# Router logits from unscaled tokens, four experts' rows gathered by rank, GpSimd products behind the bonus products

## The reference, cut to what matters

```python
x = x + y_mix @ w_out[l]
h = rms_norm_2(x, norm_ffn_w[l])          # h = x * rsqrt(mean(x^2) + eps) * w
...
g_logits = xt @ rg_w + rg_b               # 8 groups
g_sel = argmax(g_logits); g_gate = softmax(g_logits)[g_sel]
e_logits = (xt @ re_w + re_b)[group g_sel]   # 8 experts in a group
top_p, top_i = top_k(softmax(e_logits), 2)
gates = g_gate * top_p / sum(top_p)
...
hid = silu(xblk @ w_gate[e]) * (xblk @ w_up[e])    # 1024 -> 512
y = hid @ w_down[e]                                # 512 -> 1024
```

## Time and profile before

| | before |
|---|---|
| median of 3 runs | 1588.18 us (1586.01 to 1589.27) |
| the profiled execution, its own time | 1582.05 us |
| its span, first to last instruction | 1580.3 us |
| busy PE / DVE / ACT / POOL | 1154.5 / 364.5 / 218.0 / 74.7 us |
| DMA | 463.21 MB, mean 293 GB/s |

### The profile page before, as it was taken

The page is one execution under the profiler, slowest core; times in us unless marked ns, Lnnn a source line. Parts: engine busy times, 40 slices in busy tenths (PEclk is TensorE's granted clock), DMA queues, the critical chain, the costliest instruction groups (busy, mean ns, idle before and its releaser), DMA issues.

```text
span 1580.3 us, 35719 instructions
## 1 busy us (share of the span) xinstructions
PE 1154.5 (73%) x15903; PEld 839.9 (53%) x15903; DVE 364.5 (23%) x993; ACT 218.0 (14%) x600; POOL 74.7 (5%) x124
## 2 busy tenths in 40 slices
PE   7988799888998787786556655666656666665665
PEld 4867368554687574764444444444444444444443
DVE  2455024731324724311010111111111110101111
ACT  1044000530013320110000000000000000000000
POOL 1100001000100311000000000000000000000000
PEclk9996899999998889898897889888888888889888
DMA  9740136205030006699999999999999999999997
GB/s 289 278 148 1 30 110 220 80 0 191 38 107 1 2 4 247 285 375 429 429 427 430 427 429 428 429 429 427 430 426 430 427 430 428 428 429 427 430 426 324
DMA packets 68872, 463.21 MB, mean 293 GB/s; under 512 B 14645, under 2 KB 18134, under 8 KB 44246
## 3 DMA queue, kind: packets, MB, share of 16 engines
q1 hardware_dynamic: 64784, 459.76, 70.7%
q10 hardware_dynamic: 4038, 2.72, 0.6%
HBM read 461.41 MB, written 1.05 MB: 293 GB/s over the span
## 4 chain that ended last, share of the span: by engine, by line
DMA 51%; PE 7%; DVE 1%; issue 1%; ACT 0%; POOLq 0%; SPq 0%; POOL 0%; DVEq 0%
DMA weight_slots<-in_exp_w_down_dram 51%; PE bank L2150 4%; PE bank L2141 1%; PE bank L2130 1%; PE bank L2167 0%; PE bank L2111 0%; PE bank L2104 0%; ACT work_region L2081 0%; SPq L1990 0%; DVE normed_features L2277 0%; DVE normed_tokens L2216 0%; POOLq L2028 0%; DVE tokens L2331 0%; DVE normed_features L2274 0%; DVE normed_features L2248 0%
## 5 line engine op out<-in xcount | busy, mean ns | idle before, releaser
L2141 PE MATMUL bank<-weight_slots,work_region 128*32 128x128 f32 x5504 | 201.3, 308 | 130.6 <-DMA weight_slots<-in_exp_w_up_dram 102.8
L2141 PEld LDWEIGHTS bank<-weight_slots,work_region 128*32 128x32 f32 x5504 | 173.9, 124 | 157.1 <-DMA weight_slots<-in_exp_w_up_dram 113.6
L2150 PE MATMUL bank<-weight_slots,work_region 128*32 128x256 f32 x1376 | 115.0, 491 | 91.3 <-DMA weight_slots<-in_exp_w_down_dram 91.3
L2141 PE MATMUL bank<-work_region 128*32 128x128 f32 x2688 | 95.2, 302 | 62.3 <-DMA work_region<-in_exp_w_up_dram 50.7
L2150 PEld LDWEIGHTS bank<-weight_slots,work_region 128*32 128x32 f32 x1376 | 59.1, 134 | 133.3 <-issue 98.6
L2141 PEld LDWEIGHTS bank<-work_region 128*32 128x32 f32 x2688 | 82.7, 121 | 75.6 <-DMA work_region<-in_exp_w_up_dram 56.0
L2081 ACT COPY work_region<-bank 128x256 f32<-128x256 f32 x64 | 23.8, 372 | 609.5 <-PE bank L2150 609.5
L2297 DVE TENSOR_SCALAR work_region<-work_region 128x128 f32<-128x128 f32 x128 | 38.7, 345 | 294.1 <-PE bank L2158 293.0
L2308 DVE TENSOR_TENSOR work_region<-work_region,bank 128x128 f32<-128x128 f32 x64 | 23.9, 373 | 288.1 <-PE bank L2141 288.1
L2150 PE MATMUL bank<-work_region 128*32 128x256 f32 x672 | 58.0, 503 | 44.1 <-DMA work_region<-in_exp_w_down_dram 44.1
L515 PE MATMUL bank<-weight_slots,normed_features 128*128 128x512 f32 (+2 forms) x256 | 87.0, 500 | 2.2 <-DVE normed_features L701 2.2
(11 more groups left out here) (416 smaller groups left out, 1279.6 us busy)
## 6 DMA issues: line engine op xcount, KB each, us to landing
weight_slots<-in_exp_w_up_dram SPq DMA_DIRECT2D x43, 2048.0 KB, 41.0
weight_slots<-in_exp_w_down_dram SPq DMA_DIRECT2D x43, 2048.0 KB, 40.6
weight_slots<-in_exp_w_gate_dram SPq DMA_DIRECT2D x43, 2048.0 KB, 41.7
work_region<-in_exp_w_gate_dram SPq DMA_DIRECT2D x21, 2048.0 KB, 41.7
work_region<-in_exp_w_up_dram SPq DMA_DIRECT2D x21, 2048.0 KB, 41.0
work_region<-in_exp_w_down_dram SPq DMA_DIRECT2D x21, 2048.0 KB, 40.9
weight_slots<-in_w_in_dram SPq DMA_DIRECT2D x16, 2048.0 KB, 9.4
weight_slots<-in_w_out_dram SPq DMA_DIRECT2D x6, 2048.0 KB, 8.0
```

The lines of the kernel that those rows point to most:

```text
L2141: mm = nc.tensor.matmul(B[bank][BLK * j:BLK * (j + 1), 0:P], xt[u][:, c], w[u][:, c, j * P:(j + 1) * P], start=c == 0, stop=c == KC - 1, t ...
L2150: mm = nc.tensor.matmul(B[7][BLK * j:BLK * (j + 1), 0:256], hidt[u][:, BLK * k:BLK * (k + 1)], w_down[u][:, k, j * 256:(j + 1) * 256], sta ...
```

## The change

Three things are changed.

1. **Router logits.** The norm's gain is multiplied into the router's weights by GpSimd in the mixer (one more DMA, `route_gain`, on ACT's queue; one GpSimd product of 128x576 after the q and k norm). PE transposes the unscaled tokens `X` and forms the logits at the mixer's end, ahead of the barrier; `rstd` enters as a factor when DVE adds the bias. DVE still makes `XN`, now ahead of the barrier too.
2. **First four experts.** DVE forms `first_pick`, a 128x32 selection for each of the first four experts and each half of the tokens, straight from the ranks. PE gathers these 128 rows from `XN` (4 matmuls of 128x512) and transposes them (8). The sorted selection is formed later, and PE gathers the sorted list in four quarters, one behind each of the steps 0 to 3, which are written out ahead of the loop. GpSimd's windows begin at expert 4.
3. **GpSimd behind the bonus.** The two `ends` products wait for the four `rk` products, where they waited for `scaled` 5.

```diff
             inv_root(rsq, ssq, 1.0 / HD, EPS, S["qk_ss"], 1, S["qk_rstd"])
+            pool.wait_ge(mem["router_in"], 16 * N_ROUTER)
+            nc.gpsimd.tensor_tensor(w_route, w_route, shape(mem["route_gain"].unsqueeze(2), P, KC, NGROUP + NE), ALU.mult).then_inc(mem["route_ready"], 1)
...
-            pool.wait_ge(S["scaled"], 5)
+            pool.wait_ge(S["rk_ready"], CT)
             nc.gpsimd.tensor_tensor(ends(ei), ends(kx), by, ALU.mult).then_inc(S["ends_ready"], 1)
...
                 nc.scalar.activation(junk[m], X[:, m * D:(m + 1) * D], ACT.Square, accum_out=ss[:, m:m + 1]).then_inc(S["ss_ready"], 1)
+                for b in range(2):
+                    act.wait_ge(S["h_transposed"], 2 * MT + 2 * m + b + 1)
+                    nc.scalar.copy(ht[:, 4 * b:4 * b + 4, m * P:(m + 1) * P], view(B[RAW_BANK[m][b]][:, :], 4, P)).then_inc(S["ht_ready"], 1)
...
+            pe.wait_ge(mem["route_ready"], 1)
+            for m in range(MT):
+                pe.wait_ge(S["ht_ready"], 2 * MT + 2 * (m + 1))
+                for c in range(KC):
+                    nc.tensor.matmul(B[LOGIT_BANK][:, m * 72:(m + 1) * 72], ht[:, c, m * P:(m + 1) * P], w_route[:, c], start=c == 0, stop=c == KC - 1)
...
+            for m in range(MT):
+                ins = V.scalar_tensor_tensor(logit[:, m], B[5][:, m * 72:(m + 1) * 72], rstd[:, m:m + 1], b_route, ALU.mult, ALU.add)
...
+            def gather_sorted(e):
+                half, at = divmod(2 * e, 4)
+                pe.wait_ge(S["pick_ready"], MT)
+                pe.wait_ge(Q["hid_ready"], e + 1)
+                for i in range(2):
+                    for j in range(2):
+                        for m in range(MT):
+                            mm = nc.tensor.matmul(B[4 + i][:, j * T:(j + 1) * T], xn[:, m, :, 2 * (at + i) + j], sel[:, m, half * T:(half + 1) * T],
+                                                  start=m == 0, stop=m == MT - 1)
+                    mm.then_inc(Q["sorted_made"], 1)
...
             with pe.Fori(0, n):
-                step(0, 0, 1, 0, tail=False)
+                first_rows_of()
+                for e in range(FIRST):
+                    step(e, e % NBUF, e // NBUF + 1, (e - 1) // NBUF + 1, first=True)
...
+            def pick_first():
+                for m in range(MT):
+                    for e in range(FIRST):
+                        ins = V.tensor_scalar(first_pick[:, m, e], const("slot_of")[:, 0:BLK], place[:, m, e:e + 1], None, ALU.is_equal)
+                ins.then_inc(S["first_ready"], 1)
...
+                dve.wait_ge(Q["rows_made"], 2)
+                V.tensor_copy(first_rows[:, 512:], B[7][:, :]).then_inc(Q["rows_taken"], 1)
                 select(0)
+                dve.wait_ge(Q["rows_made"], 4)
+                V.tensor_copy(first_xt[:, 4:], view(B[5][:, :], 4, P)).then_inc(Q["rows_taken"], 1)
```

202 lines of the change are left out of this document (113 added, 89 removed).

## The result

| | before | changed |
|---|---|---|
| median of 4 runs | 1588.41 us (1586.01 to 1589.27) | 1572.59 us (1568.83 to 1576.35) |
| ratio, 95% interval | | 0.9898 (0.9866 to 0.993) |
| profiled execution, its span | 1582.05, 1580.3 us | 1576.35, 1574.6 us |

The change takes 15.8 us off the median; forecast were 20.2. The profiled executions lie only 5.7 us apart, so the spans can't be compared directly. Executions of one kernel scatter: in one comparison 26 executions of the kernel before ran from 1578.08 to 1597.71 us. Part of that arises ahead of the places that the change is about: VectorE's 128x2048 square of q and k comes at 418.67 us before and at 425.95 us in the changed kernel, and in eleven traces of kernels with the change or most of it anywhere from 414.07 to 428.35 us, mean 418.5.

A forecast was written before the change was run, and what follows sets the result against it. The expert weight stream bounds the kernel: its start, bytes and standstill. Start -5.2 and holes -15.0 (18.1 to 3.1) give -20.2 us, from 1588.2 to 1568.0; range 1563 to 1573, up to 1577 with the first two rivals.

The forecast's parts named there:

- Step 3: Mixer's end: router logits ahead of the barrier bring the routing 5.2 us earlier.
- Step 4: First gather: from ranks seen to expert 3's gate issue 14.6 us instead of 19.4, 4.8 earlier; VectorE's copy comes last.
- the second hole: Weight stream between the gate issues of experts 3 and 4: a standstill of 5.0 us, forecast to close.
- Step 1: Mixer: with GpSimd behind the bonus products, P4 and everything after it shift, so the stream starts 5.2 us earlier.
- rival A: Mixer: the contention only moves, GpSimd's products hold up masks and transposes, P4 starts as before; 1573.2 us, chance 0.15.
- Rival B: First gather: the first hole stays open at 8 to 10 us; 1573 to 1575 us, chance 0.15.
- Rival C: Steps 1 to 3: the sorted gather's eight matmuls ahead of the next gate product make it slower, 1593 us; chance 0.03.
- Step 2: The added GpSimd product (128x576, 1.1 us) and the DMA, ahead in the mixer, cost nothing at the end.
- one of the forecast's own signs against it: First gather: the forecast counts as wrong if VectorE's copy does not come last.
- Step 5: Routed steps: the sorted gather behind them leaves 8.3 to 9.1 us between gate products 0 and 1, gaining 5.0 us.
- The hole: Weight stream after the ninth transfer: the standstill ahead of expert 3's gate matrix shrinks from 13.1 to 3.1 us.

The follow-up runs named there:

- second comparison: The changed kernel once more against the kernel before, on another chip: 1564.92 us against 1590.06, ratio 0.9865.
- the wait for G: Changed kernel with GpSimd's `ends` products waiting for G (L1778) instead of the four bonus products; one execution: 1570.69 us beside 1596.18 of the kernel before.
- the filled kernel: Changed kernel with four unused 128x512 matmuls on TensorE between the rank counts and the first gather: 1568.93 us, ratio 0.988 to the kernel before.

## Why the prediction was right, and where it was wrong

The time lies in the range (1572.6 us, forecast 1568.0) and the direction is right. From the stream's start on the forecast was right in sum; ahead of it a whole term was wrong. Forecast were -15.0 behind the start and -5.2 ahead of it. The traces give 958.3 (mean of four of the changed kernel, with and without the move) - 973.5 (mean of three of the kernel before, likewise) = -15.2, and -0.4. The medians gave -15.8 and, in the second comparison, -25.1, with intervals that overlap between 15 and 21 us.

The terms behind the start, from the same three and four traces: the gate issue of expert 3 came 58.4 us behind it and comes at 47.4, 11.0 earlier where steps 3 and 4 were to bring 10.0; the next gate issue came 14.7 to 14.9 us later and comes 8.6 later, so that the second hole (5.0) is gone. Together that is 16.0; where the 0.8 us to the 15.2 at the end go is not shown.

**Step 1 failed as a term of the sum.** Its first half held: bonus products at 1.68 us (forecast 1.6), L1778 delayed by 1.24 (1.3), P2 4.93 us behind the start of L1447 (forecast 542.40 - 537.55 = 4.85), masks and transposes at full speed, so rival A's mechanism is wrong, although its time (1573.2) is close to the median: that is luck. The sentence that failed is "From there on PE and the others shift together". I had seen TensorE's issue wait of 1.82 us, held it for a single event and reckoned with it only as a bound on P2 and in rivals B and C. It is a series that returns after each 127 matmul records. Counted on by 127 from those four records, three of its places lie in P2 and the P4 and P8 products (after 123 records of the one, 122 and 249 of the other). In the trace of the kernel before none of the three shows (in its second trace the last, with 0.31 us), the three behind them do; during the waits for VectorE whatever supplies TensorE could catch up. In the changed kernel two of them show, 2.37 and 1.14 us, so P4 came 4.2 us earlier and not 5.2. Up to the bonus product 4.57 + 1.58 = 6.15 us of waits for VectorE are gone and the "issue" time has grown from 6.9 to 10.7 us, which leaves 2.3 of the 2.64 us that the table shows there. The rest went with the clock from the bonus product on. The count by which the idle times come, and that they take up the gain, are shown. That the clock cost the rest is read from 14 traces of one stretch, in which the same records keep TensorE busy longer; no run changed the clock by itself.

**Step 2 was right.** The added product took 1.14 us (forecast 1.1) and held VectorE's scaling of q and k beside it, L1675, 3.23 us instead of 2.29. Nothing of that is left further on: the bonus products start 117.85 to 117.92 us behind the square in every trace, with the added product and without it, but that with the wait for G (116.19).

**Step 3 was right.** The transposes ran at little over half their old time (2.10 us against 3.68). My mark, VectorE on the logits at most 28 us behind the stream's start, was met with 27.8, where 26.4 was forecast. The first half of the projection, which the step took as given, makes most of the scatter here: it took 9.91 us in this trace, 7.13 in the first of the kernel before, and 8.8 in six others. Among traces in which it took 8.8, VectorE reached the logits 33.2 to 33.4 us behind the start before and 26.7 to 26.8 now, 6.5 earlier where 5.2 were forecast. With the logits behind the barrier the end came 5.4 us later, in one trace; that undoes only a part of the step, since the tokens stay unscaled there, so it doesn't confirm the 5.2 by its number.

**Step 4 was right in sum and wrong in who is last,** one of the forecast's own signs against it. From the ranks seen (649.34) to the gate issue (663.63) are 14.3 us, in the three other traces of the changed kernel 13.7 to 13.8; forecast were 14.6, before it was 19.4. No kernel undoes this step alone. The gather started 3.6 us behind the ranks, as worked out, but took 5.87 instead of 4.2, since TensorE comes out of a wait of 3.75 us at a granted clock of 0.56 (650 to 655 us); with the wait filled it took 3.67. So TensorE and not VectorE was last: VectorE waited 1.87 us for it. That the sum came out is in part luck. The gather was 1.7 us longer than reckoned, and the gate product behind it took 2.0 us to the next issue (661.61 to 663.63), at full clock, where the sum had put it near its slow end of 2.6. In the filled kernel the two changed places: gather fast, gate product slow, same issue time.

**Step 5 was right.** The gate issues are 8.59 us apart (8.3 to 9.1), no hole follows, and the next two come after 12.2 and 11.1 us, under the 14.7 of an expert; the one behind step 3 comes after 14.7, with 1.8 us of wait for the GpSimd window at 708, and the queue is ahead. With the whole sorted gather in step 0 the gate issues are 20.1 us apart in both traces, a hole of 20.1 - 9.8 = 10.3 us, and the stream needs 8 to 11 us more. That shows that a gather in front of a gate product opens the hole; its size is for 32 matmuls, not for the 16 that stood there before. Rival C's eight matmuls took 4.2 us each time, never 8.

**The hole** was forecast at 3.1 us and is 2.7 to 4.6 in four traces. Rival B (8 to 10 us) didn't occur.

## What to carry to other kernels

Before a gain on one engine is carried through to the end, look at the engine that follows for idle time without a releaser: if it returns at a fixed number of instructions, it lies hidden beneath today's waits and takes their place when they go. Then the gain is at most what the stretch takes now less its number of such blocks times the length of one. A gain that ends at a stream of transfers (the hole in the GB/s, the next issue) can be summed to about 1 us, although single terms in it were off by more; a gain in a stretch of small matmuls has to be followed to its last product, with the granted clock of that stretch beside it. Where executions scatter by 15 us, steps of 5 us are read from the trace against a fixed point just ahead of them, not from medians.

## What the runs showed of the hardware that was not expected

- TensorE in bursts of small matmuls idles at places 127 records apart, mostly 1.1 to 2.5 us, with no semaphore behind it; with 32 more records ahead the whole series moved by 32. Idle time and products together take 3.4 to 4.1 us for 127 records; where the products are longer (127 of 32x64 in 3.63 us) the idle time shrinks to 0.3 to 0.75 us, and right behind a wait for another engine it can be nil. What fills it is not shown; the page lists a queue for instructions with 40 packets of 0.66 MB before and 44 of 0.72 MB now, 16.5 KB each.
- As forecast, a VectorE product with both inputs in SBUF was held by the GpSimd product of 1024 columns beside it: 1.93 us instead of 0.69. With an operand in PSUM, or as a transpose, it lost nothing beside the same products.
- The same stretch of work, 1081 to 1088 matmul records, took 36.1 to 41.9 us, with length times granted clock always 30.0 to 32.2.
